# Moving the second block's modulation from the first feed-forward to the second, with its products on GpSimd

## The reference

```python
for layer in range(DEPTH):                     # DEPTH = 2
    ...
    h = h + mixed @ w_mix_out[layer]
    h = h + memory_cross_attention(rms_norm(h, norm_xattn_g[layer]), mem_n, ...)
    h = h + conv_glu_ffn(rms_norm(h, norm_ffn_g[layer]), ffn_w_up[layer], ffn_conv_w[layer],
                         ffn_conv_b[layer], ffn_w_down[layer])
```

```python
cond = jax.nn.silu(c)                          # (1, 1024)
mod = cond @ w_ada[l] + b_ada[l]               # w_ada is 1024 x 6144
shift_m, scale_m, gate_m, shift_f, scale_f, gate_f = jnp.split(mod, 6, axis=-1)
h = modulate(rms_norm_2(x, g_pre_mix[l]), shift_m, scale_m)
...
```

## Time and profile before

| | |
|---|---|
| median of 3 runs | 2545.24 us |
| profiled execution, its time | 2547.41 us |
| its span, first to last instruction | 2545.6 us |
| mean granted TensorE clock | 0.954 of full speed |
| PE busy | 2354.9 us (93%) |
| DVE busy | 618.0 us (24%) |
| ACT busy | 377.7 us (15%) |
| POOL busy | 138.9 us (5%), 199 instructions |
| chain that ended last | PE 81%, DMA 11%, DVE 5% |

### The profile page before, as it was taken

One profiled execution on the slowest core, in us unless ns is written; L12 is line 12 of the kernel. 1 busy time (PEld: TensorE's weight loads), 2 busy tenths in 40 slices (PEclk: granted clock), 3 DMA queues, 4 the chain that ended last, 5 costly groups with the idle time before them and its releaser, 6 DMA issues.

```text
span 2545.6 us, 26320 instructions
## 1 busy us (share of the span) xinstructions
PE 2354.9 (93%) x11209; PEld 1535.3 (60%) x11209; DVE 618.0 (24%) x1229; ACT 377.7 (15%) x678; POOL 138.9 (5%) x199
## 2 busy tenths in 40 slices
PE   8999899999997689999999789999999999999996
PEld 5887686878876467888877664333333443333332
DVE  3434411233024232233023341111111111111112
ACT  3321111100013212100023121000000101000001
POOL 0113200000000000000000001000000010000000
PEclk9999999999998889999999679999999999999998
DMA  5210055555231311543243117999999989999994
GB/s 224 100 67 34 2 202 227 198 198 211 97 135 67 132 70 62 201 154 148 96 165 127 45 68 310 427 427 428 427 427 427 419 323 428 427 427 428 427 428 210
DMA packets 43182, 599.61 MB, mean 236 GB/s; under 512 B 5216, under 2 KB 5488, under 8 KB 6544
## 3 DMA queue, kind: packets, MB, share of 16 engines
q1 hardware_dynamic: 43056, 597.84, 57.5%
HBM read 596.77 MB, written 1.05 MB: 235 GB/s over the span
## 4 chain that ended last, share of the span: by engine, by line
PE 81%; DMA 11%; DVE 5%; ACT 1%; issue 1%; SPq 0%; PEldq 0%; DVEq 0%; ACTq 0%
PE pb L399 80%; DMA arena<-in_gu 6%; DMA kv<-in_dne 4%; PE pb L409 2%; DVE arena L301 1%; DVE arena L316 1%; ACT arena L360 1%; DMA arena<-in_dne 1%; DVE arena L308 0%; DVE arena L328 0%; DMA ring<-in_wkv 0%; ACT xt L360 0%; DMA col<-in_cols 0%; DVE arena L310 0%; DVE arena L340 0%
## 5 line engine op out<-in xcount | busy, mean ns | idle before, releaser
L399 PE MATMUL pb<-ring,arena 128*64 128x512 f32 (+2 forms) x1792 | 747.1, 607 | 48.2 <-DMA kv<-in_dne 34.0
L399 PE MATMUL pb<-arena 128*64 128x512 f32 (+10 forms) x2308 | 679.3, 464 | 22.1 <-DVE arena L301 17.1
L399 PEld LDWEIGHTS pb<-ring,arena 128*64 128x64 f32 (+2 forms) x1792 | 224.0, 138 | 518.0 <-issue 517.0
L399 PE MATMUL pb<-xt,ring 128*128 128x256 f32 (+3 forms) x1936 | 433.4, 384 | 3.6 <-DVE xt L316 3.6
L399 PEld LDWEIGHTS pb<-xt,ring 128*128 128x128 f32 (+3 forms) x1936 | 364.6, 189 | 70.0 <-issue 9.1
L399 PEld LDWEIGHTS pb<-arena 128*64 128x64 f32 (+5 forms) x2308 | 275.5, 167 | 71.0 <-issue 34.5
L399 PE MATMUL pb<-kv,arena 128*64 128x512 f32 (+2 forms) x592 | 261.3, 596 | 0.8 <-DVE arena L301 0.8
L366 ACT ACTIVATE arena<-pb 128x512 f32<-128x512 f32 (+1 forms) x143 | 81.5, 570 | 706.6 <-PE pb L409 425.5
L301 DVE TENSOR_TENSOR mix<-pb,mix 128x512 f32<-128x512 f32 x68 | 47.1, 692 | 428.8 <-PE pb L399 428.5
L360 ACT ACTIVATE arena<-arena 128x512 f32<-128x512 f32 (+6 forms) x161 | 97.9, 608 | 319.5 <-DVE arena L316 271.8
L301 DVE TENSOR_TENSOR arena<-pb,arena 128x512 f32<-128x512 f32 (+5 forms) x101 | 55.7, 552 | 298.1 <-PE pb L399 262.5
(11 more groups left out here) (168 smaller groups left out, 1907.4 us busy)
## 6 DMA issues: line engine op xcount, KB each, us to landing
ring<-in_gu SPq DMA_DIRECT2D x66, 2048.0 KB, 15.8
arena<-in_gu SPq DMA_DIRECT2D x49, 2048.0 KB, 19.6
ring<-in_dne SPq DMA_DIRECT2D x33, 2048.0 KB, 12.4
kv<-in_gu SPq DMA_DIRECT2D x17, 2048.0 KB, 19.6
arena<-in_dne SPq DMA_DIRECT2D x17, 2048.0 KB, 15.9
kv<-in_dne SPq DMA_DIRECT2D x16, 2048.0 KB, 17.7
ring<-in_up SPq DMA_DIRECT2D x14, 2048.0 KB, 8.8
ring<-in_ada SPq DMA_DIRECT2D x9, 2048.0 KB, 7.8
```

What stands on the lines that cost most here:

```text
L399: r = self.e.matmul(out, lhsT, rhs, start=start, stop=stop, skip_group_check=True)
```

## The change

1. The unit's product with `silu(c)` moves from TensorE to GpSimd (`mod_g`, new). In the weight's own slot, GpSimd multiplies all 4096 columns by the eight values of `CND`, then adds halves: 2048, 1024 and 512 columns wide. The last sum goes to `ACG`, one of four places in `arena`. Only then is the slot free.
2. TensorE sums `ACG` over its 128 partitions with four matmuls of one moving column. The copy on ACT and the matmuls with 32 weight columns are gone.
3. The place moves from `xattn 0` and `ffn 0` to `xattn 1` and `ffn 1`. GpSimd starts at `mod.c`, which DVE marks after the softmax of `xattn 1`. TensorE takes one step behind each of the 11 groups (`P.advance(1)`) and the last one ahead of `down_p`. `LOADS` has `ada.0` to `ada.11` among the loads of `wq1.1` to `up1.9`.
4. The arena's places of `xattn` and `ffn` start at 2048 in place of 1408.

```diff
 LOADS = """
-ab_small ab.0 ab.1 ab.2 ab_r.1 ab_r.0 ab_r.2 rw_scratch wkv0.0 wkv0.1 wkv0.2 wkv0.3 mixo0.0 mixo0.1 wq0.0 
-wq0.1 ada.0 ada.1 ada.2 ada.3 ada.4 wo0.0 wo0.1 up0.0 ada.5 up0.1 ada.6 up0.2 up0.3 ada.7 up0.4 ada.8 up0.5 
-up0.6 ada.9 up0.7 ada.10 up0.8 up0.9 ada.11 up0.10 dn0.0 dn0.1 dn0.2 dn0.3 dn0.4 dn0.5 dn0.6 cd.0 wkv1.0 cd.1 
-gates wkv1.1 cd_m.0 cd_m.1 cd_if wkv1.2 wkv1.3 mixo1.0 mixo1.1 wq1.0 wq1.1 wo1.0 wo1.1 up1.0 up1.1 up1.2 
-up1.3 up1.4 up1.5 up1.6 up1.7 up1.8 up1.9 up1.10 dn1.0 dn1.1 dn1.2 dn1.3 dn1.4 dn1.5 dn1.6 in2.0 in2.1 in2.2 
-in2.4 in2.3 in2.5 in2.6 out2.0 out2.1
+ab_small ab.0 ab.1 ab.2 ab_r.1 ab_r.0 ab_r.2 rw_scratch wkv0.0 wkv0.1 wkv0.2 wkv0.3 mixo0.0 mixo0.1 wq0.0
+wq0.1 wo0.0 wo0.1 up0.0 up0.1 up0.2 up0.3 up0.4 up0.5 up0.6 up0.7 up0.8 up0.9 up0.10 dn0.0 dn0.1 dn0.2 dn0.3
+dn0.4 dn0.5 dn0.6 cd.0 wkv1.0 cd.1 gates wkv1.1 cd_m.0 cd_m.1 cd_if wkv1.2 wkv1.3 mixo1.0 mixo1.1 wq1.0 ada.0
+wq1.1 ada.1 wo1.0 ada.2 wo1.1 up1.0 ada.3 up1.1 ada.4 up1.2 ada.5 up1.3 ada.6 up1.4 ada.7 up1.5 ada.8 up1.6
+ada.9 up1.7 ada.10 up1.8 ada.11 up1.9 up1.10 dn1.0 dn1.1 dn1.2 dn1.3 dn1.4 dn1.5 dn1.6 in2.0 in2.1 in2.2 in2.4
+in2.3 in2.5 in2.6 out2.0 out2.1
 """
 
 
@@ -1838,7 +1838,7 @@
 
...
-        AR.reset(1408)
+        AR.reset(2048)
         Q8 = AR.get(8, 256)
         PRB, PT = AR.get(2, 4, 256), AR.get(2, 4, 256)
         XMX, XSM = SM[:, 100:108], SM[:, 108:116]
@@ -1847,15 +1847,7 @@
         def xattn_p(P, n):
             P.begin(f"xa{n}")
             x = f"xa{n}"
-            if n == 0:
-                P.beside(mod_p(P))
-
-            def sums():
-                sum_p(P, x)
-                if n == 0:
-                    P.pace = PACE[8]
-
-            proj_p(P, f"wq{n}.0", x + ".q0", xn=x, after_first=sums)
+            proj_p(P, f"wq{n}.0", x + ".q0", xn=x, after_first=lambda: sum_p(P, x))
             proj_p(P, f"wq{n}.1", x + ".q1")
             P.wait_ge(f"free kv{n}.33")
             for i in range(2):
@@ -1883,15 +1875,16 @@
                              PT[:, mb, hd, :], mb == 0, mb == 1, sig=f"{x}.o{hd}" if d + mb == 2 else None)
             down_p(P, [MIX[:, c, :] for c in range(8)], f"wo{n}", 4, f"wo{n}",
                    ready=lambda kk: f"free {x}.o{kk // 2}")
-            P.pace = PACE[9]
 
         def xattn_s(S, n):
             S.begin(f"xa{n}")
             x = f"xa{n}"
             squares_s(S, HT, x, f"mixo{n}.h", gain=coff["xa_g"] + 8 * n)
-            if n == 0:
-                S.beside(mod_s(S))
             root_s(S, x)
+            if n == 1:
+                S.act(CND, X8, ACT.Exp, scale=-1.0)
+                sigm_s(S, CND, CND)
+                S.mark("mod.s")
             for i in range(2):
                 for h2 in range(2):
                     b = S.tile(f"{x}.s{i}{h2}")
@@ -1913,8 +1906,6 @@
         def xattn_v(V, n):
             V.begin(f"xa{n}")
             x = f"xa{n}"
-            if n == 0:
-                V.beside(mod_v(V))
             root_v(V, x)
             for u in range(2):
                 for j in (0, 2):
@@ -1932,11 +1923,15 @@
             V.recip(XSM, XSM)
             V.tt(PRB8, PRB8, bc(XSM, 2, 256), MUL)
             V.mark(x + ".p")
+            if n == 1:
+                V.wait_ge("mod.s")
+                V.tt(CND, CND, X8, MUL)
+                V.mark("mod.c")
             residual_v(V, f"wo{n}")
 
...
-        AR.reset(1408)
+        AR.reset(2048)
         AC = AR.get(22, 256)
         CB2 = [AR.get(2, 256) for _ in range(2)]
         UB = AR.get(2, 256)
@@ -1946,6 +1941,8 @@
         def ffn_p(P, n):
             P.begin(f"ffn{n}")
             f = f"f{n}"
+            if n == 1:
+                P.beside(mod_p(P))
             for g, (w2, tiles) in enumerate(FFN):
                 w = P.unit(f"up{n}.{g}")[:, 0:16 * w2].rearrange("p (k n) -> p k n", k=8)
                 names = [f"{f}.u{g}", f"{f}.g{g}"]
@@ -1961,7 +1958,8 @@
                 P.used(f"up{n}.{g}")
                 for name in names:
                     P.release(name)
-            if n == 0:
+                P.advance(1)
+            if n == 1:
                 P.drain("mod.d")
             down_p(P, FBLOCKS, f"dn{n}", 4, f"dn{n}", ready=lambda kk: f"{f}.ac{kk}", merged=3)
 
@@ -1978,12 +1976,12 @@
                     S.act(cb[0:cw, q, :], cb[0:cw, q, :], ACT.Silu)
                     S.mark(f"{f}.s{g}{q}")
             S.table(LNEXP)
-            if n == 0:
-                S.fill("mod.d")
 
         def ffn_v(V, n):
             V.begin(f"ffn{n}")
             f = f"f{n}"
+            if n == 1:
+                V.beside(mod_v(V))
             root_v(V, f)
 
             def fc(name, at, cw):
@@ -2013,9 +2011,8 @@
                     V.wait_ge(f"{f}.s{g}{q}")
                     V.tt(AC[0:cw, g * 2 + q, :], UB[0:cw, q, :], cb[0:cw, q, :], MUL)
                     V.mark(f"{f}.ac{g * 2 + q}")
-            if n == 0:
+            if n == 1:
                 V.fill("mod.d")
-            else:
                 V.memset(BG, 0.0)
                 V.mark("mo.bg")
             residual_v(V, f"dn{n}")
@@ -2023,62 +2020,41 @@
 
 
         AR.reset(0)
-        CB, ST = AR.get(8, 32), AR.get(2, 512)
+        ACG = AR.get(4, 512)
         CND = SM[:, 116:124]
         X8 = COL[:, coff["cond"]:coff["cond"] + 8]
 
+        def mod_g(G):
+            G.begin("mod")
+            G.wait_ge("mod.c")
+            for n in range(12):
+                w = G.unit(f"ada.{n}")[:, :].rearrange("p (k n) -> p k n", k=8)
+                G.tt(w, w, bc(CND, 2, 512), MUL)
+                G.tt(w[:, 0:4], w[:, 0:4], w[:, 4:8], ADD)
+                G.tt(w[:, 0:2], w[:, 0:2], w[:, 2:4], ADD)
+                if n > 3:
+                    G.wait_ge(f"mod.a{n - 4}")
+                G.tt(ACG[:, n % 4, :], w[:, 0, :], w[:, 1, :], ADD)
+                G.used(f"ada.{n}")
+
         def mod_p(P):
-            P.m.put("due mod", P.steps + 1)
-            yield True
+
             for n in range(12):
-                u = f"ada.{n}"
-                name = f"mod.a{n}"
-                b = P.side_tile(name)
-                w = P.unit(u)[:, :].rearrange("p (k n) -> p k n", k=8)
-                P.wait_ge("mod.c")
-                for c in range(8):
-                    P.mm(b[32 * (c % 4):32 * (c % 4) + 32, :], CB[:, c, :], w[:, c, :], c < 4, c >= 4,
-                         sig=name if c == 7 else None)
-                    if c == 3:
-                        yield True
-                P.used(u)
-                P.side_done(name)
+                b = P.side_tile(f"mod.a{n}")
+                P.wait_ge(f"used ada.{n}")
+                for q in range(4):
+                    P.mm(b[:, q:q + 1], ACG[:, n % 4, q * 128:(q + 1) * 128], ones[:, 0:1], True, True,
+                         sig=f"mod.a{n}" if q == 3 else None)
+                P.side_done(f"mod.a{n}")
                 yield True
-                name = f"mod.b{n}"
-                b = P.side_tile(name)
-                P.wait_ge(f"free mod.a{n}")
-                for q in range(4):
-                    P.mm(b[:, q:q + 1], ST[:, n % 2, q * 128:(q + 1) * 128], PICK, True, True,
-                         sig=name if q == 3 else None)
-                P.side_done(name)
-                yield True
-
-        def mod_s(S):
-            yield S.due_at("mod")
-            S.act(CND, X8, ACT.Exp, scale=-1.0)
-            sigm_s(S, CND, CND)
-            S.mark("mod.s")
+
+        def mod_v(V):
             for n in range(12):
-                yield S.due_at(f"mod.a{n}")
-                b = S.got(f"mod.a{n}")
-                S.copy(ST[:, n % 2, :], b)
-                S.free(f"mod.a{n}")
-
-        def mod_v(V):
-            yield V.due_at("mod")
-            V.wait_ge("mod.s")
-            V.tt(CND, CND, X8, MUL)
-            V.copy(CB, bc(CND, 2, 32))
-            V.memset(PICK, 0.0)
-            for q in range(4):
-                V.memset(PICK[32 * q:32 * q + 1, :], 1.0)
-            V.mark("mod.c")
-            for n in range(12):
-                yield V.due_at(f"mod.b{n}")
-                b = V.got(f"mod.b{n}")
+                yield V.due_at(f"mod.a{n}")
+                b = V.got(f"mod.a{n}")
                 o = coff["b_ada"] + 4 * n
                 V.tt(MODC[:, 4 * n:4 * n + 4], b[:, 0:4], COL[:, o:o + 4], ADD)
-                V.free(f"mod.b{n}")
+                V.free(f"mod.a{n}")
             V.stt(CA, MODC[:, 8:16], 1.0, gain_of("g_pre_mix"), ADD, MUL)
             V.tt(CA, CA, gain_of("final_g"), MUL)
             V.tt(CG1, MODC[:, 16:24], gain_of("g_post_mix"), MUL)
@@ -2944,6 +2920,7 @@
             G.wait_ge("load const16")
             front_g(G)
             rwkv_g(G)
+            mod_g(G)
             moe_g(G)
             rounds(G, lambda r: None)
 
```

## The result

The changed kernel takes **2560.15 us**, the median of 5 runs (2559.05 to 2567.22); the kernel before took 2545.24 us in the same comparison (2542.5 to 2546.05). The ratio is 1.0066, with a 95% interval from 1.0051 to 1.0081: slower by 15 us. The profiled execution took 2559.05 us, with a span of 2557.0 us and a mean granted clock of 0.95, against a span of 2545.6 us before, so the two traces differ by 11.4 us and the medians by 14.9.

A forecast was written before the change was run, and what follows sets the result against it. TensorE's own time was taken to bound both layers (97.7% and 97.6% busy). -40 us in layer 0 and +65 in layer 1 gave +25: 2572 from the profiled 2547.4, less 2.2 for the median, 2570 us; range 2540 to 2598.

The forecast's parts named there:

- main case: Whole kernel: DVE and GpSimd taking turns at their port make it slower, 2570 us, own range 2553 to 2585; 66%.
- What is taken away: Layer 0's query, attention and feed-forward stretch loses the modulation's matmuls on TensorE: -40.1 us.
- Step (a): Trace sign: layer 0 from first query matmul to first `down` matmul takes about 239 us.
- What GpSimd has to do: GpSimd in layer 1: one product and three sums make a 15.5 us unit; 12 units take 186 us.
- The second rival: GpSimd's product with `CND` costs as much per column as the sums: 9.4 us, kernel at 2590 us; 12%.
- the third: Whole kernel comes out even, with a 13.8 us unit and six shared DVE instructions: 2545 us; 8%.
- The port: Layer 1 feed-forward: DVE and GpSimd alternate, one whole instruction each; eight shared DVE instructions a group, some 0.45 us each.
- step (c): Trace sign: DVE's multiply-adds in `ffn 1` average several us until GpSimd's last unit, 0.5 us after it.
- Early groups: Layer 1 feed-forward: eight DVE turns, about 32 us, put group 2 at 1093; 34 us more put group 3 at 1127.
- step (d): Trace sign: TensorE waits for DVE about 8 and 19 us ahead of groups 2 and 3, then some 5 each to 8.
- Later groups: Layer 1 feed-forward: groups 3 to 7 take 20 us each against 13.9 before; group 8 starts at 1225, `down` at 1270.
- The first rival: DVE is let in during GpSimd's long instructions and waits little: `down` at 1219, kernel at 2519 us; 14%.

The follow-up runs named there:

- run 4: Changed kernel without GpSimd's product and two wide sums (modulation then wrong); loads, slots, marks and TensorE's steps stay: 2517.8 us, ratio 0.9891 to the kernel before.
- run 1: Changed kernel with DVE's working value UB in a free PSUM bank in the second feed-forward, GpSimd's work untouched: 2520.11 us, ratio 0.9897 to the kernel before.
- run 2: Control: the kernel before, with UB in PSUM in the second feed-forward and GpSimd idle there: 2547.33 us, ratio 1.0001.
- run 3: Changed kernel with GpSimd's 4096-column product cut into four and its 2048-column sum into two pieces of 1024: 2536.15 us, ratio 0.9954 to the kernel before.
- run 5: Changed kernel with GpSimd's product in eight pieces of 512 columns and its two wide sums in four and two: 2539.7 us, ratio 0.9982 to the kernel before.
- the repeat of run 1: The kernel of run 1, unchanged, timed again later on another chip: 2523.02 us, ratio 0.9915 to the kernel before.
- run 6: Changed kernel with DVE's product for `mod.c` moved ahead of the softmax, just behind `root_v`, so GpSimd may start earlier: 2554.7 us, ratio 1.0038 to the kernel before.

## Why the prediction was right

The direction and the mechanism were right, and 2560.15 us lies in the main case's own range. By the steps of the prediction:

- *What is taken away*, 40.1 us: measured 40.6. Step (a) expected 239 us, the window is 238.64.
- *TensorE's steps*, +11 us: 11.4 us in run 4 against the kernel before. Right.
- *What GpSimd has to do*: 15.5 us a unit, measured 15.52 alone. The product took 7.02 us where I had 7.2 (step b). The second rival needed 9.4 us and falls with that; the third needed a unit of 13.8 us and free scales, and had neither. The figure of the Trainium skill for it (GPSIMD Engine Reference, "Elementwise — side-by-side cycle accounting"), 4.5 us for two inputs of 2048 columns, is what the wide sum took, 4539 ns, but the product with its repeated input is faster per column.
- *What is queued behind it*: `wo1.1` 3 us late. It was 4.00 us late, and the matmuls behind it took 1.8 us more than 13.98 in a window with a granted clock of 0.89. I had counted no clock there.
- *The port*: DVE's multiply-adds in layer 1 had a mean of 2.6 us until GpSimd's last unit and took 0.5 after it, step (c). Runs 1 and 2 show the cause: with one operand moved to PSUM the cost is gone, and without GpSimd the move is worth nothing. Run 3 shows the rule, turn for turn. The Trainium skill (SBUF — State Buffer, "Who interferes with whom") says that the shared pair is held for the whole instruction and that the other engine fully blocks; the trace now agrees up to a 7 us instruction (7.12 us for one multiply-add at 1044.99). The scales from SBUF took up to 6.08 us, so they are shared too.
- *Early groups*: TensorE waited 8.34 us ahead of group 2, as expected, and that is partly luck. DVE's first shared instruction came 101.2 us after the first query matmul and not 95.8: `wo1.1` and the slow matmuls behind it had cost 5.8 us, and the prediction's 1062 left out even its own 3 us for `wo1.1`. But the first eight turns took 29 us and not 31. The next eight took 25 us where I had 34, so group 3 began at 1077.90 - 922.65 = 155 us and not at 161, behind a wait of 7.68 us where step (d) had 19.
- *Later groups*: step (d) had a wait of some 5 us ahead of each. There were two, 6.47 and 3.15 us ahead of groups 6 and 7, and next to none ahead of 4, 5 and 8: while GpSimd waited (3.12 us for TensorE's step until 1094.67, 6.72 and 5.83 us for loads until 1102.66 and 1155.78) DVE went at its own speed. The pace of groups 3 to 8 was to be 19.7 us and was (1168.89 - 1077.90)/5 = 18.2.
- **The term that was mis-sized** is the length of a turn, in two ways. The first is what a DVE turn costs GpSimd. I had 0.4 us, near the 0.33 us that a 0.79 us product took from it in the earlier trace rows; measured are 0.05 us for DVE's 0.5 us instructions (run 3), and 15.71/4 = 3.93 us a turn in the changed kernel in place of 4.25. The second is that each shared instruction was to wait for a whole GpSimd instruction. Between the shared ones DVE does others that never wait, and so it can come in the middle of an instruction (the pair at 1053.01) or find the way free: the second eight turns took 3.1 us each. Together the sixteen turns were 11 us shorter than forecast, which less the later start is the 5.6 us at group 3. GpSimd ended 205 us after its start and not 214: DVE's turns cost it about 1 us and not 16, while its waits for loads and for TensorE's steps were 17.4 us and not 12. Groups 3 to 8 were 7.5 us faster than forecast, and the last three took 46.3 us in place of 44.5. That makes 5.6 + 7.5 - 1.8 = 11.3 us, against 65 - 53.4 = 11.6: -40.6 + 53.4 is +12.8 and not +25.
- *The range*: its lower bound, 2553, came from a 13.8 us unit with turns of the forecast's cost. The unit was as forecast and the turns were shorter, so that 2560 is in the main case's range is in part luck.
- *The first rival's break-even*: `down` at 1245 is a pace of 14.7 us from group 3 at 1127, and not 16.
- *The expert stage*, step (f): 1024.8 and 1025.2 us. Right.

The first rival's number, 2519, is what run 1 gives (2520.11): the steps, the late `wo1.1` and its slow matmuls are all that is left when the groups' instructions wait for nothing. Its mechanism, that DVE would be let in during GpSimd's long instructions, is not what happens.

Three things stay open. The old TensorE modulation in the new place wasn't tried, so engine and place are separated only by the sum above. What makes the clock fall is not settled: in the changed kernel the groups behind waits of 3.15 us and more are slow and the others not, and run 3's, behind 2.1 us each, are all at full clock, but in run 5 groups behind 2.18 and 1.60 us took 17.00 and 15.77 us, soon after one of 3.74, and in the repeat of run 1 the first 64 records of `down` took 15.74 us behind a wait of 0.52, where run 1 took 14.05. No run varied the waits alone. Nor does a run show why a short DVE turn costs GpSimd so much less than its own length.

## What to carry to other kernels

Before work goes to an idle GpSimd, count in the trace the DVE instructions that run beside it and have both inputs in SBUF, and the scales and copies from SBUF to SBUF: each may wait for one whole GpSimd instruction, so DVE may lose up to their number times GpSimd's mean length (3.9 us here; 3.6 and 3.1 us a turn were measured in the two groups counted above), whatever its busy share says. The bottleneck engine pays what goes beyond DVE's slack. Two cheap edits take the price away: put one operand in PSUM, and cut GpSimd's instructions until DVE's turns fit into the time it has, but no further than GpSimd's own total allows. When a wait is removed and the time stays, look for the next place where the two engines meet.

## What the runs showed that I had not expected

- GpSimd loses almost nothing to DVE's short instructions: 0.05 us a turn, against several us for DVE. To a DVE product of 2048 columns it lost 1.95 us (run 6).
- The product with a repeated input takes 7.02 us for 4096 columns in one instruction and 8.88 us in eight; with DVE's turns between, 9.1 to 9.4.
- The granted clock is part of the price of a wait: of the 53.4 us, 9.2 us behind the waits for DVE and 1.8 us behind the wait for `wo1.1` are TensorE in part at the lower level.
- A DVE operation on two columns, from SBUF to SBUF, waits as well: 3.76 us in run 6 in place of 0.17.
